# Loading the first expert table in 16 pieces a block from one queue instead of 4 from two

## The reference

```python
def peer_block(xb, w_pq, sub_keys, u_tab, v_tab):
    q = (xb @ w_pq).reshape(T, PEER_HEADS, 2, D_HALF)
    s = jnp.einsum('thcd,ckd->thck', q, sub_keys).astype(jnp.float32)
    ...
    eidx = jnp.take_along_axis(cidx, sel, axis=-1)
    g = jax.nn.softmax(best, axis=-1)
    u = jnp.take(u_tab, eidx, axis=0)
    a = jax.nn.gelu(jnp.einsum('thkd,td->thk', u, xb).astype(jnp.float32))
    vv = jnp.take(v_tab, eidx, axis=0)
    return jnp.einsum('thk,thkd->td', (g * a).astype(xb.dtype), vv)
```

## Time and profile before

| what | us |
|---|---|
| median of 3 runs | 2699.69 (2693.34 to 2713.22) |
| the profiled execution | 2700.05 |
| its span | 2698.4 |
| first transpose of the first table's stage starts | 878.07 |
| last transpose of it starts | 1891.78 |
| last gelu of it starts | 1914.21 |

### The profile page before, as it was taken

The page is one execution under the profiler, slowest core; times in us unless marked ns, Lnnn a source line. Parts: engine busy times, 40 slices in busy tenths (PEclk is TensorE's granted clock), DMA queues, the critical chain, the costliest instruction groups (busy, mean ns, idle before and its releaser), DMA issues.

```text
span 2698.4 us, 37865 instructions
## 1 busy us (share of the span) xinstructions
PE 2442.0 (90%) x13838; PEld 2180.1 (81%) x13838; DVE 1920.3 (71%) x2105; ACT 931.3 (35%) x1018; POOL 1175.7 (44%) x684
## 2 busy tenths in 40 slices
PE   5988889889799999999979988899999989998999
PEld 4867768668699999999978878899877777787777
DVE  4554544543546998989867676777587888888888
ACT  4353543522322333323323222223333333333333
POOL 1020100120000001068788888883576676767662
PEclk9999999989899999999999998899999999999999
DMA  5453443467264668789989999998899999999997
GB/s 196 125 172 109 149 134 110 158 247 286 68 133 109 168 167 228 204 213 217 209 222 249 236 237 231 226 238 222 297 395 378 396 407 392 394 407 385 394 400 298
DMA packets 271975, 661.38 MB, mean 245 GB/s; under 512 B 64953, under 2 KB 114937, under 8 KB 229720
## 3 DMA queue, kind: packets, MB, share of 16 engines
q1 hardware_dynamic: 150736, 334.56, 39.2%
q0 software_dynamic: 82064, 249.26, 27.5%
q10 hardware_dynamic: 39095, 76.57, 11.2%
HBM read 613.65 MB, written 46.02 MB: 244 GB/s over the span
## 4 chain that ended last, share of the span: by engine, by line
PE 31%; POOL 26%; DMA 19%; DVE 12%; issue 8%; ACT 2%; DVEq 1%; SPq 0%; ACTq 0%; POOLq 0%
POOL g_dense L493 17%; PE banks L1291 9%; PE banks L1292 9%; PE banks L1293 9%; POOL a_values L535 6%; DVE h L1243 4%; DMA g_dense<-route,route_place 3%; DMA a_tile<-a_dense 3%; DMA v_row<-in_v_tab,route_place 3%; DMA raw<-in_v_tab 3%; DMA k_cache<-in_cache_k 2%; DMA v_raw<-in_v_tab 2%; POOL u_row L487 2%; DVE u_turned L1120 2%; POOL v_row L526 1%
## 5 line engine op out<-in xcount | busy, mean ns | idle before, releaser
L1291 PE MATMUL banks<-xT_hi,ring_hi 128*128 128x320 f32 (+1 forms) x2304 | 736.6, 320 | 92.8 <-DVE ring_lo L1124 85.5
L1292 PE MATMUL banks<-xT_lo,ring_hi 128*128 128x320 f32 (+1 forms) x2304 | 730.3, 317 | 0.0
L1293 PE MATMUL banks<-xT_hi,ring_lo 128*128 128x320 f32 (+1 forms) x2304 | 729.5, 317 | 0.0
L493 POOL DMA_INDIRECT g_dense<-route,route_place x256 | 494.9, 1933 | 140.8 <-issue 74.1
L1291 PEld LDWEIGHTS banks<-xT_hi,ring_hi 128*128 128x128 f32 x2304 | 443.5, 193 | 104.1 <-issue 92.8
L1292 PEld LDWEIGHTS banks<-xT_lo,ring_hi 128*128 128x128 f32 x2304 | 444.0, 193 | 0.0
L1293 PEld LDWEIGHTS banks<-xT_hi,ring_lo 128*128 128x128 f32 x2304 | 443.1, 192 | 0.0
L526 POOL DMA_INDIRECT v_row<-in_v_tab,route_place x128 | 279.6, 2185 | 182.7 <-DVE h L1243 159.2
L861 DVE TENSOR_TENSOR ring_lo<-raw,ring_hi 128x2048 fp32r<-128x2048 f32 x72 | 164.6, 2291 | 264.8 <-ACT ring_hi L573 264.5
L1120 DVE STREAM_TRANSPOSE u_turned<-raw 128x2048 f32<-128x2048 f32 x128 | 295.6, 2310 | 71.6 <-DMA raw<-in_u_tab 61.6
L1243 DVE SCALAR_TENSOR_TENSOR h<-v_row,w_values,h 128x2048 f32<-128x2048 f32 x128 | 300.4, 2347 | 42.7 <-DMA v_row<-in_v_tab,route_place 39.8
(11 more groups left out here) (219 smaller groups left out, 3869.5 us busy)
## 6 DMA issues: line engine op xcount, KB each, us to landing
raw<-in_u_tab SPq DMA_DIRECT2D x256, 256.0 KB
raw<-in_u_tab ACTq DMA_DIRECT2D x256, 256.0 KB
v_raw<-in_v_tab SPq DMA_DIRECT2D x64, 1024.0 KB
raw<-in_v_tab SPq DMA_DIRECT2D x64, 1024.0 KB
raw<-in_w_in SPq DMA_DIRECT2D x160, 256.0 KB
a_dense<-gelu_out SPq DMA_DIRECT2D x128, 160.0 KB
raw<-in_w_out SPq DMA_DIRECT2D x64, 256.0 KB
g_dense<-zeros POOLq DMA_DIRECT2D x16, 1024.0 KB, 26.2
```

The costliest lines, as they stand in the source:

```text
L493: pool.indirect_dma_start(out=places, out_offset=bass.IndirectOffsetOnAxis(ap=routeU[:, t, 2, j:j + 1], axis=0), in_=route[:, t, 0, j:j + ...
L1291: MM(out, h1, h2, start=first, stop=False)
L1292: MM(out, h1, l2, start=False, stop=False)
L1293: return MM(out, l1, h2, start=False, stop=last)
```

## The change

Each block is loaded by 16 DMAs of 32 partitions and one piece of 2 KB (64 KB) instead of 4 of 32 partitions and four pieces (256 KB). All 16 are issued by SP, in the order of pieces r = 0 to 3 and, within a piece, quarters 0, 2, 1, 3. ScalarE issues none. Quarters 0 and 2 add to `raw_ready[k]`, quarters 1 and 3 to a new semaphore `raw_odd[k]`, and the transpose waits for both.

```diff
+        raw_odd = [sem("raw_odd0"), sem("raw_odd1")]
...
-        def u_quarter(m, k, a):
-
-            return (raw[32 * a:32 * a + 32, k, :].rearrange("p (q r d) -> p q r d", r=4, q=1), u_v[a, :, ds(m, 1), :, :])
+        def u_piece(m, k, a, r):
+
+            return (raw[32 * a:32 * a + 32, k, r * W:(r + 1) * W].rearrange("p (q d) -> p q d", q=1), u_v[a, :, ds(m, 1), r, :])
...
             def u_weights(m, k):
 
-                load(m, k, [u_quarter(m, k, a) for a in range(2)], (u_turn, m + 1))
+                sp.wait_ge(u_turn, m + 1)
+                for r in range(4):
+                    for a in (0, 2, 1, 3):
+                        sp.dma_start(*u_piece(m, k, a, r)).then_inc((raw_odd if a % 2 else raw_ready)[k], 16)
...
-            def u_upper(m, k):
-
-                for a in (2, 3):
-                    act.dma_start(*u_quarter(m, k, a)).then_inc(raw_ready[k], 16)
-
             def u_hi(m, k):
                 act.wait_ge(u_turn, m + 3)
-                if m + 2 < P:
-                    u_upper(m + 2, k)
                 act.wait_ge(split_used, m + (BASE_U + 1))
...
-            act.wait_ge(u_turn, 2)
-            u_upper(0, 0)
-            u_upper(1, 1)
             u_hi(0, 0)
...
             def turn(m, k):
-                dve.wait_ge(raw_ready[k], m * 32 + (64 * (BASE_U // 2 + 1) - 32 * k))
+                dve.wait_ge(raw_ready[k], m // 2 * 128 + (64 * (BASE_U // 2) + 128))
+                dve.wait_ge(raw_odd[k], m // 2 * 128 + 128)
                 dve.wait_ge(lo_done, m + (BASE_U + 1))
```

## The result

The changed kernel takes 2850.56 us (median of 4 runs, 2847.43 to 2854.22) and the kernel before 2697.68 us in the same runs: a ratio of 1.054, 95% interval 1.051 to 1.058. It is 153 us slower. The forecast was 2870 us with a range of 2765 to 2965.

A forecast was written before the change was run, and what follows sets the result against it. SP's DMA issues were to become the first stage's bound, at 9.5 us a block against 7.98. Last transpose 180.0 us late, less 8.4 us in the tail, gives 171.6 on 2700: 2872, stated as 2870 us, range 2765 to 2965.

The forecast's parts named there:

- parts 1 and 2: SP's loop in the first table's stage: 14 more issues make its cycle 9.5 us (8.6 to 10.3), above 7.98.
- I: Interval on SP from one DMA issue's start to the next, address work included: taken as 0.52 us, 0.46 to 0.58.
- part 3: Six blocks ahead of SP's loop: 96 issues take 40.3 us, loop starts at 912.1; last transpose 180 us late.
- part 4: Tail of the first stage: 14.0 us from last transpose to last gelu instead of 22.4, giving back 8.4 us.
- part 5: ACT no longer issues upper halves: worth 0 here, at most 56.7 us if SP were no bound.
- part 6: Transpose's added wait on a second semaphore: costs nothing of its own.
- part 7: Gelu stores behind 16 SP issues: up to 7.3 us later, buffer needed two blocks (19 us) later, cost 0.
- part 8: Second table's stage: starts later, otherwise the same, its 800 us set by DMA at 0.97 busy.
- Rival A: SP's issues in the first stage: at most 0.41 us each, cost hidden, 2700 us within 1%; chance 0.06.
- Rival C: SP's issues back up: two of sixteen take 1.06 us, cycle 10.6 us, time 3005 us; chance 0.10.
- Rival B: First table's transfers get quicker by mixing quarters; VectorE's 59.2 us wait for raw goes, 2641 us; chance 0.04.
- 74% busy: Sign in the first stage: TensorE waits some 2 us in each block and is 74% busy.

The follow-up runs named there:

- the eight: Changed kernel with two pieces to a DMA, eight DMAs of 128 KB a block from SP, order 0, 2, 1, 3: 2685.11 us, 0.9935; timed again 0.9939.
- the twelve: Changed kernel with pieces 0 and 1 in one DMA, twelve DMAs a block from SP: 2692.88 us, ratio 0.997.
- the run with the store in the middle: Changed kernel with SP's wait and gelu store between pieces 0, 1 and pieces 2, 3 of a block's loads: 2860.30 us, ratio 1.058.

## Why the prediction was right, point by point

**The bound (parts 1 and 2).** Right. SP's cycle was forecast at 2.2 + 14 x I and is 9.2 us. I was taken as 0.52 and is 0.50 to 0.51, near the pairs of 0.82 us and the loads of w_pq; the pairs of 0.90 us, which I had averaged in, mostly did not carry over. That 0.52 came so close is in part luck: my reason for taking less than 0.54 was wrong, since the issue of 32 pieces takes 316 ns, like that of 128. The term was 0.3 us a block too large, 36 us over 121 cycles, which by itself would put the last transpose at 2036; it started at 2043.08, against 2071.8 forecast, for the next reason.

**The blocks ahead of the loop (part 3).** Mis-sized the other way: the first loads of the loop started at 918.19 us, not 912.1, since 80 issues took 38.55 us, 0.48 each instead of 0.42. The last transpose then was 151.3 us late, where I said 180.

```profile
870.90 38.55 SPq L351 DMA_DIRECT2D raw<-in_u_tab  x80
...
918.19 7.82 SPq L351 DMA_DIRECT2D raw<-in_u_tab  x16
```

**What follows the last transpose (part 4).** Mis-sized: 20.5 us, where I said 14.0, so 1.9 us came back and not 8.4. Two of TensorE's blocks were still to do, not one: the last two gelus are 7.04 us apart. My chain had the wrong order on VectorE, where the transpose of block m + 1 stands ahead of the ring_lo of block m; so the ring_lo of the last block but one began only behind the last transpose, and TensorE's last block but one with it.

```profile
2045.32 2.25 DVE L1119 TENSOR_TENSOR ring_lo<-u_turned,ring_hi 128x2048 fp32r<-128x2048 f32 x1
```

**ACT without its issues (part 5).** Worth 0, and the run with four DMAs from SP shows it even where SP is no bound: 0.999.

**The second semaphore (part 6).** It was not tried alone. The eight and the twelve wait for it too and are no slower than the kernel before, so it costs nothing that shows.

**The stores (part 7).** The cost of 0 was right, but not what I said of the cover. I counted two blocks until the buffer is needed, and ACT waited 775 us. The release of a buffer (L361) stands behind the loads of the block after, so it comes when SP has issued sixteen more. That this wait cost nothing is shown by the run with the store in the middle.

**The second stage (part 8).** From the last gelu to the end it took 789.0 us against 784.2; I had said unchanged, and 10 us as the limit. The profiled executions of the other versions have 789.1 us (four from SP), 778.4 (eight in the order 0, 1, 2, 3) and 791.4 (twelve), so 4.8 us is no more than their spread.

The sum was 171.6 us; measured in the profiled execution 154.2 us. The mechanism was right, and the closeness is partly luck: the cycle was sized 36 us too dear, and the start of the loop, the tail and the second stage together some 17 us too cheap. **Rival A** fell with I = 0.50 us. **Rival C** too: issues that back up did occur, but the longest of 2048 took 1.15 us, and the cycle stayed 9.2. **Rival B** can only be judged where SP keeps up. Its first step is right: mixing and a finer cut do make the transfers cheaper for the DMA engines, 0.92 to 0.84. The rest does not follow. VectorE's wait for raw falls from 59.2 us to almost nothing with the eight (905 to 1890 us; 13.4 us when timed again):

```profile
DVE u_row L1191 <- DMA u_row<-in_u_tab,u_index: 111.2, 18, 12.9
...
DVE u_turned L1116 <- DMA raw<-in_u_tab: 6.9, 6, 2.4
```

But it was down to 12.8 us already with four DMAs in the old order, all from SP, where the DMA engines were busy 0.92 and the time was that of before. So most of this wait went with ACT's issues and not with cheaper transfers. Before, ACT came to its two issues of a block 2.9 us on average behind SP's two, and the last of them 5.5 us behind (1886.4 against 1880.9, and the earlier trace rows); that this was the wait is likely, but no run separates it. Nor did the time fall with the wait: that for gathered rows of u_row rose from 88.7 us to 115.7 with the four and to 111.2 and 95.4 in the two profiles of the eight. The mistake in the 59 us of rival B was to count a wait as time. What makes the eight 17 us faster, and what bounds the stage in that version, stays open.

Of TensorE I had said 74% busy. It was busy 944.48 of 1135 us (905 to 2040 us), 83%. I had divided 7.05 us by a cycle of 9.5; the cycle was 9.2, and 48 matmuls of a block counted as busy for 944.48 / 5933 x 48 = 7.6 us, where by the earlier trace rows it was 923.73 / 6045 x 48 = 7.3 before. The granted clock was 0.94 on average against 0.96, which goes the same way; how much of the difference it makes was not worked out.

## What to carry to other kernels

Count what a queue issues in a loop, not only what it moves: add up the issue time per iteration of the instruction queue that starts the DMAs, compare it with the iteration, and cut transfers finer only as far as that sum stays under it. Here SP's waits in the trace before (5.3 us a block) over 0.50 us gave the room in advance: some ten issues more than its two, and twelve fitted while sixteen did not. A second queue gives room too, but not for nothing if its engine has work of its own: eight issues on ACT kept ring_hi back by 3.4 us. Eight DMAs of 128 KB in the mixed order have the lowest time of the versions run, 0.6% under before; the interval of the twelve overlaps with theirs.

## What the runs showed of the hardware that I had not expected

An issue on SP costs the same for 32 pieces as for 128 (316 and 317 ns), and back to back with nothing in between it stretches to 422 ns, so that 0.46 to 0.48 us an issue is what SP reached at best over sixteen.

The Trainium skill says that the time the sequencer takes to initiate a DMA is "usually small relative to the DMA itself" ("DMA: Bandwidth & Descriptors", section "Issuing engines are not separate DMA queues"). With four DMAs a block the runs agree: moving all of them to one queue changed nothing (0.999). With sixteen they don't. From 905 to 2040 us the DMA engines carried 191 GB/s at 0.74 busy, by which 64 KB take some 0.25 us of their time, an estimate; the issue took 0.50 us. The measurement decides: at 64 KB SP brought 1 MB in 9.2 us, 114 GB/s of the table, less than the 131 GB/s of a block in 7.98 us before.

The other thing was how much the order of the quarters and the cut take off the DMA engines, 0.92 to 0.84 of the stage for the same bytes, and how little of that came out as time.
